# A two-layer hybrid trunk on one core: the norm and the units around it in token halves

## The reference

```
h = rms_norm(x, norm1_g) * (1 + sc1) + sh1
z, xbc, dt_raw, q, k, v, gate_s, gate_a = split(h @ w_in)
y_ssm = mamba2(z, xbc, dt_raw) @ w_ssm_out
y_att = diff_attention(q, k, v) @ w_attn_out
x = x + g1 * ((sigmoid(gate_s) * y_ssm + sigmoid(gate_a) * y_att) @ w_out)
h = rms_norm(x, norm2_g) * (1 + sc2) + sh2
x = x + g2 * (square(relu(h @ w_ff1)) @ w_ff2)
```

## Time and profile before

| what | value |
|---|---|
| median of three runs | 2412.51 us |
| lowest, highest | 2404.48, 2412.53 us |
| span of the profiled execution | 2406.6 us |
| its own total | not recorded beside the span |
| TensorE matmul busy | 2307.6 us, 96% |
| VectorE (DVE) busy | 1376.5 us, 57% |
| GpSimd busy | 1106.4 us, 46% |
| ScalarE busy | 1012.4 us, 42% |
| mean granted TensorE clock | 0.981 |

### The profile page before, as it was taken

The page is one execution under the profiler, slowest core; times in us unless marked ns, Lnnn a source line. Parts: engine busy times, 40 slices in busy tenths (PEclk is TensorE's granted clock), DMA queues, the critical chain, the costliest instruction groups (busy, mean ns, idle before and its releaser), DMA issues.

```text
span 2406.6 us, 32072 instructions
## 1 busy us (share of the span) xinstructions
PE 2307.6 (96%) x11800; PEld 1924.0 (80%) x11800; DVE 1376.5 (57%) x2041; ACT 1012.4 (42%) x1862; POOL 1106.4 (46%) x825
## 2 busy tenths in 40 slices
PE   7999998999999989999989999999999998999997
PEld 6788997887778868888877789988777786888886
DVE  6677675466653567777757777612666534321324
ACT  2456652355553232322334666433555433332332
POOL 2466553534434434444534655554344444444442
PEclk9999999999999989999999999999999998999998
DMA  6333334522224235545422333232121232222221
GB/s 252 102 93 117 99 93 155 186 71 66 67 71 147 98 129 199 184 169 203 153 97 86 114 104 110 76 102 95 62 71 62 76 117 88 88 97 96 97 97 52
DMA packets 94125, 267.19 MB, mean 111 GB/s; under 512 B 8528, under 2 KB 35536, under 8 KB 88592
## 3 DMA queue, kind: packets, MB, share of 16 engines
q1 hardware_dynamic: 84656, 248.22, 30.5%
q10 hardware_dynamic: 9312, 16.91, 2.5%
HBM read 260.77 MB, written 4.33 MB: 110 GB/s over the span
## 4 chain that ended last, share of the span: by engine, by line
issue 38%; PE 25%; POOL 16%; POOLq 14%; DVE 2%; DMA 1%; PEld 1%; ACT 1%; DVEq 1%; ACTq 0%; SPq 0%; PEldq 0%
POOL w_lo L1796 15%; POOLq L1798 14%; PE gemm L554 4%; PE gemm L556 4%; PE gemm L555 4%; PE gemm L577 2%; PE gemm L578 2%; PE gemm L579 2%; PE aux L728 2%; PE aux L619 1%; PE aux L739 1%; PE aux L744 1%; POOL smalls L1784 1%; DMA ada_pe<-stream 1%; PEld aux L606 1%
## 5 line engine op out<-in xcount | busy, mean ns | idle before, releaser
L1796 POOL TENSOR_TENSOR w_lo<-raw,w_hi 128x512 fp32r<-128x512 f32 x704 | 978.2, 1410 | 1201.7 <-ACT w_hi L922 1192.8
L922 ACT ACTIVATE w_hi<-raw 128x1024 fp32r<-128x1024 f32 x352 | 371.4, 1058 | 739.8 <-PE gemm L556 623.5
L554 PE MATMUL gemm<-h_hi,w_hi 128*128 128x512 f32 x1504 | 607.6, 404 | 5.5 <-DVE h_lo L1362 5.0
L556 PE MATMUL gemm<-h_hi,w_lo 128*128 128x512 f32 x1504 | 592.5, 394 | 0.0
L555 PE MATMUL gemm<-h_lo,w_hi 128*128 128x512 f32 x1504 | 592.5, 394 | 0.0
L554 PEld LDWEIGHTS gemm<-h_hi,w_hi 128*128 128x128 f32 x1504 | 287.4, 191 | 66.8 <-issue 10.5
L556 PEld LDWEIGHTS gemm<-h_hi,w_lo 128*128 128x128 f32 x1504 | 286.5, 190 | 62.2
L555 PEld LDWEIGHTS gemm<-h_lo,w_hi 128*128 128x128 f32 x1504 | 287.3, 191 | 58.7 <-issue 1.9
L554 PE MATMUL gemm<-op_hi,w_hi 128*128 128x512 f32 x608 | 238.6, 392 | 0.2
L556 PE MATMUL gemm<-op_hi,w_lo 128*128 128x512 f32 x608 | 236.8, 389 | 0.0
L555 PE MATMUL gemm<-op_lo,w_hi 128*128 128x512 f32 x608 | 236.6, 389 | 0.0
(11 more groups left out here) (191 smaller groups left out, 3341.2 us busy)
## 6 DMA issues: line engine op xcount, KB each, us to landing
raw<-stream SPq DMA_DIRECT2D x336, 512.0 KB
ada_late<-stream SPq DMA_DIRECT2D x30, 1024.0 KB, 4.9
seg<-decay_rows ACTq DMA_DIRECT2D x64, 256.0 KB, 3.4
ada_early<-stream SPq DMA_DIRECT2D x40, 256.0 KB, 4.1
raw<-stream SPq DMA_DIRECT2D x32, 256.0 KB
ada_first<-stream SPq DMA_DIRECT2D x5, 1024.0 KB, 20.8
x<-xT SPq DMA_DIRECT2D x2, 2048.0 KB, 10.2
ada_pe<-stream SPq DMA_DIRECT2D x3, 1024.0 KB, 14.2
```

The costliest lines, as they stand in the source:

```text
L554: mm(o, w_hi[:, slot, k, cols], hi[:, k, :], start=k == 0, stop=False)
L556: last = mm(o, w_lo[:, slot, k, cols], hi[:, k, :], start=False, stop=k == KB - 1)
L922: A(w_hi[:, slot, ks], raw[:, slot, ks], ACT.Copy).then_inc(hi_ready, 1)
L1796: gp.tensor_tensor(w_lo[:, slot, ks], raw[:, slot, ks], w_hi[:, slot, ks].bitcast(F32), ALU.subtract)
```

## The change

The unit that ends at a norm is now done for tokens 0 to 255 (side 0) with both column halves, and then for tokens 256 to 511 (side 1), each side in a PSUM bank of its own. All steps of the norm exist once for each side, at 256 tokens. TensorE's sum and spread of side 0 stand inside the matmuls of side 1. The units behind the norm are done by sides too: at a mix norm the first two feed-forward units (both for side 0, then both for side 1), at the boundary and at the start the first unit with the dt projection. DVE takes the x update, the sum and the mean of side 1 between the blocks of side 0; ScalarE takes the squares of side 1 and the conversions of the second unit there. GpSimd takes both roots ahead of the low halves of the second unit. The output is written for two blocks and one side at a time.

```
+SIDES = [slice(0, S // 2), slice(S // 2, S)]
+X_PARTS = [(k, slice(0, S)) for k in range(KB - 2)] + [(k, side) for side in SIDES for k in (KB - 2, KB - 1)]
-        COLUMN_UNITS = (U_WO + N_WO - 1, UNITS - 1)
+        SPLIT_UNITS = (U_WO + N_WO - 1, UNITS - 1)
...
+            def unit_side(slot, k, side, hi, lo):
+                cols = SIDES[side]
+                for j in range(2):
+                    o = gb[2 * slot + j][:, cols]
+                    ws = slice(j * P, (j + 1) * P)
+                    mm(o, w_hi[:, slot, k, ws], hi[:, k, cols], start=k == 0, stop=False)
+                    mm(o, w_hi[:, slot, k, ws], lo[:, k, cols], start=False, stop=False)
+                    last = mm(o, w_lo[:, slot, k, ws], hi[:, k, cols], start=False, stop=k == KB - 1)
+                if side and k in (KB // 2 - 1, KB - 1):
+                    last.then_inc(gemm_done, 1)
+
+            def unit_split(l, n, hi, lo, step):
+                slot = n % 2
+                open_half(l, n, 0)
+                open_half(l, n, 1)
+                for side in range(2):
+                    cols = SIDES[side]
+                    for j in range(2):
+                        o = gb[2 * slot + side][:, SIDES[j]]
+                        ws = slice(j * P, (j + 1) * P)
+                        for k in range(KB):
+                            if side and k == KB // 2 + 1:
+                                if j == 0:
+                                    norm_sum(step, 0)
+                                else:
+                                    norm_spread(step, 0)
...
+                    last.then_inc(gemm_done, 1)
...
@@ TensorE, dt projection and first unit of a layer
+                for side in range(2):
+                    cols = SIDES[side]
+                    for k in range(KB):
+                        if l and side == 0 and k == KB // 2 + 1:
+                            norm_sum(st, 1)
+                        pe.wait_ge(S_["h_lo"], st.at("h_lo", side * KB + k) + 1)
...
+                        unit_side(0, k, side, h_hi, h_lo)
+                    if l and side == 0:
+                        norm_spread(st, 1)
@@ TensorE, mix norm
+                unit_split(l, U_WO + N_WO - 1, h_hi, h_lo, st)
+
+                for side in range(2):
+                    for u in range(2):
+                        for k in range(KB):
+                            if side == 0 and k % (KB // 2) == 0:
+                                open_half(l, U_FF + u, k // (KB // 2))
+                            if u == 0:
+                                if side == 0 and k == KB // 2 + 1:
+                                    norm_sum(st, 1)
+                                pe.wait_ge(S_["h_lo"], st.at("h_lo", side * KB + k) + 1)
+                            unit_side(u, k, side, h_hi, h_lo)
+                        if side == 0 and u == 0:
+                            norm_spread(st, 1)
@@ ScalarE
+                normed_high(st, lambda k: ada_v[:, 3, k:k + 1],
+                            {(0, 3): lambda: last_squares(st), (0, 5): lambda: convert(l, U_FF + 1, 0),
+                             (0, 7): lambda: convert(l, U_FF + 1, 1)})
@@ DVE
+            def closing_norm(l, n, step, gain, mul, shift, x_ends):
+                last_x(l, n, 0, gain)
+                norm_add(step, (KB - 2, KB - 1))
+                norm_total()
+                norm_mean(step, 0)
+                def x_end():
+                    last_x(l, n, 1, gain)
+                    x_ends()
+                def sum_end():
+                    norm_add(step, (KB, KB + 1))
+                    norm_total()
+                norm(step, 0, mul, shift, {3: x_end, 5: sum_end, 7: lambda: norm_mean(step, 1)})
+                norm(step, 1, mul, shift, {})
@@ GpSimd
             def rsqrt_of_x(step):
-                pool.wait_ge(S_["ms"], step("ms") + 1)
-                power(ms, rs).then_inc(S_["rs"], 1)
+                for side in range(2):
+                    cols = slice(2 * side, 2 * side + 2)
+                    pool.wait_ge(S_["ms"], step.at("ms", side) + 1)
+                    gp.tensor_tensor(rs[:, cols], ms[:, cols], half[:, cols], ALU.pow).then_inc(S_["rs"], 1)
...
-                for n in range(U_AO + 1, U_FF + 2):
+                for n in range(U_AO + 1, U_FF + 1):
                     low_unit(l, n)
                 rsqrt_of_x(st)
-                for n in range(U_FF + 2, UNITS):
+                for n in range(U_FF + 1, UNITS):
```

More of the change, by code:

```diff
@@ L515, in sp_program @@
                     load_dtw(l + 1)
-            for k in range(KB):
-                sp.wait_ge(S_["pre"], DEPTH * TOTAL["pre"] + k + 1)
-                sp.dma_start(out[:, k], y_out[:, k]).then_inc(out_done, 16)
+            for side in range(2):
+                for k in range(0, KB, 2):
+                    sp.wait_ge(S_["pre"], DEPTH * TOTAL["pre"] + side * KB + k + 2)
+                    sp.dma_start(out[:, k:k + 2, SIDES[side]], y_out[:, k:k + 2, SIDES[side]]).then_inc(out_done, 16)
             sp.wait_ge(out_done, KB * 16)
@@ L584, in unit @@
                 slot = n % 2
[L585 to L592, removed]
                 for k in range(KB):
@@ L965, in act_program @@
             act.wait_ge(x_in, 16)
-            squares_of_x(Step(0, "start"), range(KB), False)
+            squares_of_x(Step(0, "start"), range(len(X_PARTS)), False)
             for l in range(DEPTH):
@@ L1346, in scales, with norm @@
                 settle()
-            def norm(step, mul, shift):
-                b = full(step, 1)
+            def norm(step, side, mul, shift, between):
+                cols = SIDES[side]
+                if side:
+                    dve.wait_ge(aux_full[0], step.at("bank0", 2) + 1)
+                else:
+                    dve.wait_ge(aux_full[1], step.at("bank1", 0) + 1)
+                b = ab[1 - side]
                 for k in range(KB + 1):
+                    if k in between:
+                        between[k]()
@@ L1364, in norm, with last_x @@
+                        STT(h_lo[:, k - 1, cols], pre[:, (k - 1) % 2, cols], shift(k - 1),
+                            h_hi[:, k - 1, cols].bitcast(F32), ALU.add, ALU.subtract).then_inc(S_["h_lo"], 1)
                         settle()
+            def last_x(l, n, side, gain):
+                dve.wait_ge(gemm_done, done_at(l, n, side))
+                cols = SIDES[side]
+                for j in range(2):
+                    k = KB - 2 + j
+                    last = STT(x[:, k, cols], gb[2 * (n % 2) + side][:, SIDES[j]], gain(k), x[:, k, cols], ALU.mult, ALU.add)
+                    if j:
+                        last.then_inc(bank_free[n % 2], 1)
+                    dve.drain().then_inc(S_["xb"], 1)
@@ L1395, in dve_program @@
                     scales(0)
-                else:
-                    norm_mean(st)
-                norm(st, lambda k: amul[:, k:k + 1], lambda k: ada_v[:, 0, k:k + 1])
+                    for side in range(2):
+                        norm(st, side, lambda k: amul[:, k:k + 1], lambda k: ada_v[:, 0, k:k + 1], {})
+                else:
+                    take_ada(5, l, ab[3], 5 * KB, 5 * KB, 6 * KB)
                 dve.wait_ge(S_["lam"], st.at("lam", 1) + 1)
```

204 lines of the change are left out of this document (104 added, 100 removed).

## The result

The changed kernel takes 2413.48 us (median of 17 runs, 2410.41 to 2419.12), the kernel before 2410.33 (17 runs, 2404.48 to 2414.20); the ratio is 1.0019 with a 95% interval of 1.0011 to 1.0026. The forecast was 2405.4 from a median of 2412.5. The sign was wrong, though the time lies in the range: 7.1 us less were forecast, and 3.2 us more came out, a miss of some 10 us.

The account below looks back on a forecast made before the run. TensorE sets the time and stops at the norms. Mix norms -11.4, boundary +2.7, start +0.6, dt chain +1.0, end 0 sum to -7.1 us: 2405.4 from 2412.5; 2401 to 2410 at 50%, eight in ten 2396 to 2416.

Parts of the forecast that it names:

- Other edits cost nothing: Moved x save and loads, ada bias and GpSimd's boundary low halves: no cost; up to 2 us if that cover went.
- Mix norms: Norm unit through second unit behind it: 49.1 us becomes 42.8; 5.7 saved each after the clock, 11.4 for two.
- second unit starting on GpSimd, not DVE: Sign at mix norms: the second unit waits another 0.8 us for GpSimd's first low half, ready at 25.4 to 25.9.
- a mean of 0.6 for the clock: Charge per mix norm for half clock after several short TensorE waits close together, range 0 to 1.7 us.
- Boundary: Layer boundary: DVE's small operations make TensorE wait 5.05 us inside the unit; loss 2.7 us, range 0 to 5.
- Start: First norm, unit and dt projection: extra DVE steps and narrow matmuls lose 0.6 us together, range 0 to 2.
- dt chain: Later TensorE wait for DVE's dt chain, 4.7 us in both layers, grows by about 0.5 each: +1.0.
- end: Last unit to final writes: 27.4 us before and after, so nothing, -0.5 to +1; outputs of 0.49 us apiece.
- A: Rival: everything hides at the norms, mix norm 37.5 us, boundary 31.7; 2379 us in all; 6%.
- B: Rival: narrow matmuls pace at half a wide one, 0.1133 us, so 528 pairs lose nothing; 2398.3 us; 20%.
- C: Rival: half clock stays through both low sides, +5.1 us a mix norm, +3 at the boundary; 2418.6 us; 12%.
- D: Rival: boundary wait, mix-norm clock, start and dt chain each cost twice the charge, nearly no effect; 2410.9 us; 12%.

Follow-up runs that it names:

- e1: The changed kernel, with DVE doing layer 0's third late ada piece ahead of the first feed-forward unit's products instead of behind them; 2405.52 us, ratio 0.9987.
- e9: e3 with e5's wide start, e6's early spread and, at the boundary alone, GpSimd's low halves held until DVE finishes side 0; 2395.33 us, ratio 0.9943.
- e6: e3, with TensorE at the boundary spreading side 1's roots ahead of block 7 of side 0 instead of behind it; 2402.64 us, ratio 0.9978.
- e8: e3, with GpSimd's low halves of the second unit held at mix norms and boundary until DVE's last low part of side 0; 2398.36 us, ratio 0.9954.
- e2: The changed kernel, with DVE doing the next layer's small operations (biases, scales, dt weights, parameters) one unit earlier at the boundary; 2407.36 us, ratio 0.9994.
- e5: e3, with layer 0's first norm, its unit and the dt projection back at 512 columns; 2400.21 us, ratio 0.9968.
- e3: The changed kernel with the edits of both e1 and e2; 2401.38 us, ratio 0.9969 to the kernel before.

## Why the prediction was wrong

**The failing step: the sum ends a mix norm with the second unit behind it, and puts what comes after at nothing ("Other edits cost nothing").** The list under these words has the x save, the moved ada bias and GpSimd's low halves at the boundary; DVE's ada piece behind the mix norm of layer 0 isn't in it, and no row was read for it. (The prediction's "start of the second unit behind it" is a slip: its 49.1 us are 2014.55 to 2052.77 and one more unit, so they end with that unit.) The two feed-forward units end 5.8 us apart instead of 10.9, so GpSimd's low halves, DVE's products and its ada piece fall together, and the unit behind the norm pays 7.9 us. e1 takes just that away (7.8 in the stretch, 8.0 in the time). The row to ask was that of TensorE's ada sum in the kernel before: a cover of 3.9 us, against a lead of which the regrouping alone takes 5.1. The forecast of 2405.4 stands beside 2405.52 for e1, and that closeness is luck: the forecast started from a median of 2412.51, which 17 runs put at 2410.33, and against the kernel before e1 is only 0.13%, or 3 us, faster, where 7.1 were forecast. The rest of the miss of 12.9 in the table is 2.7 at the mix norms, 1.4 at the boundary, 0.9 at the start and 1.6 between the stretches, less 1.6 at the end.

**Mix norms: the mechanism right, the size short.** Forecast, with the unit's start as 0, and in brackets the time in the trace of the changed kernel and what it makes from that start: DVE takes side 0 at 6.0 (845.67, 5.95), sum at 8.25 (848.00, 8.28), spread at 11.7 (851.42, 11.7), next unit at 13.95 (853.76, 14.04). The wait in the unit was 0.57. From then on the gaps of TensorE, from start to start, were 1.5, 1.5 and 2.05 ahead of blocks 2, 4 and 6, DVE's loop being the bound as said with a pitch of 0.97 (pre at 855.91, 856.88). The miss is the stretched low parts (1.9 us: 3.00 for 1.07), in part made good by a root of 0.69 us for two columns instead of my 1.0 and by the 0.8 us of waiting for GpSimd's first low half, which never came: that half was ready at 25.3, about as forecast, but TensorE by then was late (27.0). So the sign I had named, "second unit starting on GpSimd, not DVE", failed. Layer 0 won 5.0 at full clock, for 6.3 forecast at full clock. In layer 1 the waits are the same to 0.01 us, but the clock fell at the last block of side 0 (2051.18), and 3.7 were won. I had charged a mean of 0.6 for the clock; the difference of the two norms is 1.3, and in the six other runs of this order both norms pay for the clock four times, one of them once (e9) and none once (e6).

**Boundary: the mechanism right, the size short by 1.4.** The wait inside the unit was forecast at 5.05 from DVE's backlog and is 5.1; in all 4.1 were lost for the 2.7 forecast, within the range of 0 to 5. The forecast had DVE hide nearly under TensorE in side 0; TensorE waited there 0.8, 0.7 and 1.4 us, the last for the same two low parts of 3.01 us beside GpSimd (with GpSimd held back it is 0.3 in e8 and e9). Seen in advance, the big wait was still taken for a price of the change, when it was a price of the order: e2 takes the loss away with one digit.

**Start, dt chain and end.** The start lost 1.5 (forecast 0.6, with the range to 2): 1.0 for the narrow matmuls (the prediction writes "2 x 0.97", but 72 pairs at 0.0134 are 0.97 once), 1.2 for the late starts told under e5, less 0.7 for a slow beginning that was shorter this time. The growth of the wait for DVE's dt chain, 0.5 in each layer, didn't come: it is 4.53 us in both layers before and 4.55 and 4.54 after. What the table shows between the stretches, 1.2 and 1.4, has nothing to do with it. The end won 1.6 (forecast 0): outputs of 256 columns follow each other every 0.40 us, 3.22 for eight, not 0.49 each, the last writes land 2.5 and not 3.1 us behind DVE, and the root is short.

```profile
2406.64 3.22 DVE L1418 SCALAR_TENSOR_TENSOR y_out<-x,con,aux 128x256 f32<-128x256 f32 x8 [1.52 <-PE aux L657]
```

**Rivals.** A (all hidden) is far off: DVE's loop bounds side 0 as said. B (narrow matmuls at half a wide one) is refuted: at full clock they start 0.12 apart in all the stretches above. C (half clock through both low sides) isn't what happened: the mix norm of layer 0 ran at 1.00, and in layer 1 the clock fell only at the end of the first low side. D came nearest in time (2410.9) and named the wrong places. The range to 2416 held it, the order that decided was in none of them.

**What stays open.** Between the stretches of the table the two traces drift apart and together again by 1 to 2 us where the matmuls of one run at half clock and those of the other don't, for instance behind TensorE's waits of 2.2 us in the attention. Runs of one kernel spread by some 10 us, so effects under 2 us rest on single traces, and these on the clock that each happened to get. Why the clock fell in one mix norm and not in another with the same waits is open.

## What to carry to other kernels

When units are regrouped so that two of them end close together, follow every in-order engine past the region that was changed, to the point where its lead is back to what it was; here the price sat in the first unit behind it. For each piece of work that an engine does "on the side", write down when it is ready and when it is taken, before and after: a cover of 3.9 us doesn't survive the loss of 5.1. And before an operation is moved ahead of another on GpSimd, look at what DVE does beside it: with two SBUF inputs it pays for each. Last, before a gain of a microsecond is read from two traces, compare the granted clocks of the two stretches: here the clock alone made up to 1.5 us at a mix norm (45.65 in e1, 44.11 in e6) and 2.7 at the boundary (e3 and e5).

## What the runs showed of the hardware

GpSimd's power on 128x2 takes 0.69 us, on 128x4 1.01: half the columns for two thirds of the time. DVE's two-input low part of 256 columns takes 0.48 alone and 0.94 to 1.5 beside GpSimd's subtraction, while the one with a PSUM input stays at 0.48. TensorE did not lose its clock over a mix norm of 44 us in which it was busy for 38.2, with gaps up to 2.05 us, in layer 0, and did in layer 1 with the same gaps. In the kernel before two waits of 2.20 us in the attention, alike in what stands around them, ended at 545.77 and 609.80: the 3.2 us behind the first have a granted clock of 0.61, those behind the second 1.00.
